# A three-block fp32 kernel: mixing in pieces, and the sparse attention's buffers, norm and last output moved to other steps

## The chip, the cores and the metric

The program runs on one core of one Trainium2 chip. Its time is the device time of one execution in microseconds (us). Before the change the median of three runs is 3529.36 us (3528.5 to 3529.94). The engines are TensorE (PE, with PEld for its weight loads), VectorE (DVE), ScalarE (ACT), GpSimd (POOL) and SyncE (SP, which issues the weight DMAs). Each runs its own instruction list in order, and they meet at semaphores.

## The reference, cut to what matters

```python
# first block, one layer: x is 512 x 1024
za, zb, zc, xbc, dt_raw, g_raw = split(rms_norm(h) @ w_in)
u, v  = split(gelu(za)); v = layer_norm(v)
ya    = u * (einsum('gts,bcsgd->bctgd', tril(w_s), v) + b_s)      # "mixing", 8 groups
yb    = gelu(gate) * scan(a, inp)   # a = exp(-8 * r * softplus(-lambda)), the "rate"
merged = gates[0] * (ya @ w_a) + gates[1] * (yb @ w_b) + gates[2] * (yc @ w_c)
# second block, two layers
x = x + 0.5 * swiglu(rms_norm(x), ffn1)
a_val, a_gate, b_gate, c_gate, b_h, q, k, v, q_idx, k_idx, w_idx = split(rms_norm(x) @ w_in)
y_a = silu(layer_norm(conv31(a_val * sigmoid(a_gate))))
y_b = b_gate * conv3(c_gate * b_h)
y_c = sparse_attention(q, k, v, top 128 keys of the indexer)     # 8 heads, 4 blocks of 128 queries
x = x + concat(y_a, y_b, y_c) @ w_out
x = x + cross_attention(rms_norm(x), rms_norm(mem))              # 256 memory rows, wk and wv from mem
x = x + 0.5 * swiglu(rms_norm(x), ffn2)
```

## The kernel before, in words

**Weights and panels.** Activations lie in SBUF with features on the partitions and the 512 positions along the row. Every weight matrix is worked off in panels of 128 output features. A panel is 24 matmuls (8 tiles of the contraction, three products each: high part by high part, high by low, low by high, since each fp32 value is held as two fp32r values). Two panels are a pair; `PHASES` lists all pairs in order. For panel k of the next pair ACT copies `raw` to `w_hi` (`prep`, L1183) once PE is through with panel k of this pair, and DVE forms `w_lo` (`prep_lo`, L1895). Before a panel PE waits for `w_lo` (`s_wlo`) and for the bank (`s_free`). So DVE has one panel of time for `w_lo`, less what ACT takes, and all its other work stands in order around these two steps.

**Buffers.** `xn_hi/xn_lo` hold a normed input, `y_hi/y_lo` an inner activation (in the first block the roles are the other way round; `b_hi/b_lo` is `xn`). `small`, `stat`, `rstd` and `arena` hold the rest. PSUM has the banks `G[0..3]` for panels and `B[0..3]` for other products.

**The gating phase.** The phases `u` (4 pairs, the half u of `za`), `lru0`, `lru1`, `ga0`, ... follow each other. `gmlp_norm(at_)` puts the layer norm of v beside the panels of `u` on DVE (variances at panel 3, division at 5, the tiles at 5 and 6). After the pair `lru0` PE runs `mix()` (L787): eight groups of four products. DVE turns each into `ya` with `mixed()`: an add (L2215), a product with u (L2220), ACT's copy of the high part (L1422), and the low part (L1910). Then DVE works out the recurrence's rate in small operations (`lru_rate`). POOL issues the DMA of the weights `lru_w` (L2569) when the low part of group 7 is done, since `lru_w` takes the place of u in the arena. PE's `lru_gates(0)` (L798) follows the pair `lru1` and waits for that DMA.

**The sparse attention.** Both layers run `MIX`, 22 panels of `w_in`, and beside them the indexer, the selection of keys for the blocks 1 and 2 (MAX8 and MATCH_REPLACE8 on DVE) and the taps of the convolution (product on ACT L1045, add on POOL L2582). Then comes a loop of 32 steps (4 query blocks by 8 heads), in `dsa_pe`, `dsa_act` and `dsa_dve`. In step i PE does the scores of step i+3 (L541), half a panel of the memory's keys or values (`half_kv`, L826, 12 matmuls), the output of step i (L581) and the transposes of the probabilities of step i+1 (L673). DVE does the maximum (L1774), `w_lo` in even steps and, until step 13, the selection for block 3; ACT does the exponential (L1078), `w_hi` in even steps and copies (L1089). Around this stand:
- the normed memory (`mem_hi` L1052, `mem_lo` L1753; 8 tiles each), at the start of the loop;
- per query block `out_tok` (L1787, DVE), `turn_out` (PE's transposes of it, L673, at head 1 of the next block), `out_hi` (L1129, ACT) and `out_lo` (L1910, DVE);
- the layer norm of the convolution: sums over channels in PE at step 19 and 21 (L553), the mean on DVE at step 20 (L1759 to L1764), square root on ACT at 23, reciprocal on DVE at 24 (L1827), Silu and high part on ACT at 25 (L1111, L1115), low part at 26.

After the loop the pairs of `w_out` (`mwo`) run as plain panels on `y_hi/y_lo`.

## Time and profile before

| | |
|---|---|
| median of 3 runs | 3529.36 us |
| profiled execution | 3529.81 us, span 3527.7 us |
| TensorE busy in the span | 3422.6 us (97%) |
| VectorE, ScalarE, GpSimd busy | 1958.6, 1360.1, 203.7 us |
| DMA | 310.29 MB, mean 88 GB/s |
| granted TensorE clock, mean | 0.989 of full speed |

The profile is one execution. Busy times are of instructions that compute. "L684" is line 684 of the kernel. A row of an instruction names what it writes, then what it reads, and behind its count the idle time before it and what ended that idle time. "PEclk" is the share of full speed that the clock of TensorE had in a stretch: 1.00 is 2.4 GHz, 0.50 is 1.2 GHz.

### The profile page before, as it was taken

The page shows a single profiled execution, that of the slowest core. Times are in us where ns is not written, and L with a number is a line of the kernel's source. Part 1 is how long each engine was busy: PE and PEld are TensorE (multiplying, and loading weights), DVE is VectorE, ACT ScalarE, POOL GpSimd, SP SyncE. Part 2 cuts the span into 40 slices and gives each one's busy share as a digit, 9 for nine tenths or more (in the row PEclk, how much of TensorE's full clock was granted, in tenths as well). Part 3 has the DMA queues.
Part 4 walks back from the last instruction along what each step waited for, and adds up shares of the span by engine and source line. Part 5 has one row for each costly group of instructions (what it writes and reads, how often), then busy time and mean ns, then how long its engine had stood idle before and what let it go on. Part 6 is the DMA issues. An engine that isn't in the chain of part 4 may idle for free.

```text
span 3527.7 us, 42389 instructions
## 1 busy us (share of the span) xinstructions
PE 3422.6 (97%) x15684; PEld 2783.7 (79%) x15684; DVE 1958.6 (56%) x2679; ACT 1360.1 (39%) x1915; POOL 203.7 (6%) x158
## 2 busy tenths in 40 slices
PE   7999999999999999999899999999999989999999
PEld 5778777888888888877678888888887777778887
DVE  4677765564446545588544544454446884454444
ACT  4455444432224342346534322342223564342223
POOL 1000000000000000045100000000000640000000
PEclk9999999999999999999999999999999999999999
DMA  4332312232223333322221333333333221223332
GB/s 129 94 84 84 96 48 72 96 111 96 95 96 96 96 95 96 90 84 72 72 72 60 96 95 96 90 101 96 98 94 89 84 72 60 72 72 95 96 96 83
DMA packets 425595, 310.29 MB, mean 88 GB/s; under 512 B 17256, under 2 KB 423200, under 8 KB 425440
## 3 DMA queue, kind: packets, MB, share of 16 engines
q1 hardware_dynamic: 422880, 302.13, 28.6%
q0 software_dynamic: 1664, 4.52, 0.4%
q8 instruction: 101, 1.65, 0.2%
q10 hardware_dynamic: 896, 1.54, 0.1%
q14 instruction: 54, 0.44, 0.0%
HBM read 306.06 MB, written 2.10 MB: 87 GB/s over the span
## 4 chain that ended last, share of the span: by engine, by line
PE 88%; DVE 8%; ACT 2%; issue 2%; DMA 0%; ACTq 0%; POOL 0%; DVEq 0%
PE G L684 75%; PE G L844 2%; PE G L826 2%; DVE arena L1744 1%; DVE w_lo L1895 1%; DVE small L1743 1%; PE B L673 1%; PE G L623 1%; PE B L604 1%; PE B L541 1%; PE B L581 1%; ACT w_hi L1183 1%; PE G L858 1%; PE G L673 0%; PE G L525 0%
## 5 line engine op out<-in xcount | busy, mean ns | idle before, releaser
L1183 ACT ACTIVATE w_hi<-raw 128x1024 fp32r<-128x1024 f32 x579 | 613.6, 1060 | 1523.3 <-PE G L684 1449.5
L1895 DVE TENSOR_TENSOR w_lo<-raw,w_hi 128x1024 fp32r<-128x1024 f32 x580 | 718.5, 1239 | 712.5 <-ACT w_hi L1183 710.0
L684 PE MATMUL G<-xn_hi,w_hi 128*128 128x512 f32 x2272 | 895.7, 394 | 12.1 <-DVE w_lo L1895 12.1
L684 PE MATMUL G<-xn_hi,w_lo 128*128 128x512 f32 x2272 | 885.8, 390 | 0.0
L684 PE MATMUL G<-xn_lo,w_hi 128*128 128x512 f32 x2272 | 885.4, 390 | 0.0
L684 PE MATMUL G<-y_hi,w_hi 128*128 128x512 f32 x1888 | 745.0, 395 | 3.4 <-DVE w_lo L1895 2.4
L684 PE MATMUL G<-y_hi,w_lo 128*128 128x512 f32 x1888 | 736.2, 390 | 0.0
L684 PE MATMUL G<-y_lo,w_hi 128*128 128x512 f32 x1888 | 735.7, 390 | 0.0
L684 PEld LDWEIGHTS G<-xn_hi,w_hi 128*128 128x128 f32 x2272 | 427.2, 188 | 118.2 <-issue 23.6
L684 PEld LDWEIGHTS G<-xn_lo,w_hi 128*128 128x128 f32 x2272 | 427.2, 188 | 91.3 <-issue 4.1
L684 PEld LDWEIGHTS G<-xn_hi,w_lo 128*128 128x128 f32 x2272 | 427.1, 188 | 89.7
L684 PEld LDWEIGHTS G<-y_hi,w_hi 128*128 128x128 f32 x1888 | 355.2, 188 | 85.9 <-issue 7.9
L684 PEld LDWEIGHTS G<-y_lo,w_hi 128*128 128x128 f32 x1888 | 355.2, 188 | 75.1 <-issue 2.9
L684 PEld LDWEIGHTS G<-y_hi,w_lo 128*128 128x128 f32 x1888 | 354.8, 188 | 74.6
L2582 POOL TENSOR_TENSOR arena<-arena,temps 128x512 f32<-128x512 f32 x90 | 132.3, 1483 | 1901.3 <-ACT temps L1045 1901.3
L1919 DVE SCALAR_TENSOR_TENSOR h<-G,h 128x512 f32 (+1 forms) x88 | 60.8, 691 | 254.8 <-PE G L684 254.8
L2025 DVE TENSOR_TENSOR temps<-G,rstd 128x512 f32<-128x512 f32 x88 | 60.8, 691 | 192.3 <-PE G L684 192.3
L1232 ACT ACTIVATE temps<-temps 128x512 f32<-128x512 f32 x88 | 55.6, 632 | 185.4 <-DVE temps L2021 185.4
L1936 DVE SCALAR_TENSOR_TENSOR h<-G,h 128x512 f32<-128x512 f32 x80 | 55.3, 691 | 120.6 <-PE G L684 112.5
L826 PE MATMUL G<-xn_hi,w_hi 128*128 128x256 f32 x256 | 84.9, 332 | 4.1 <-DVE xn_lo L1753 4.1
L1910 DVE TENSOR_TENSOR y_lo<-temps,y_hi 128x512 f32 (+1 forms) x124 | 83.5, 685 | 3.5 <-ACT y_hi L1235 3.1
L1235 ACT ACTIVATE y_hi<-temps 128x512 f32 (+1 forms) x88 | 55.7, 633 | 58.3 <-DVE temps L2028 58.3
(368 smaller groups left out, 3123.4 us busy)
## 6 DMA issues: line engine op xcount, KB each, us to landing
raw<-in_w_in SPq DMA_DIRECT2D x128, 512.0 KB, 4.3
raw<-in_ffn_w_gate SPq DMA_DIRECT2D x88, 512.0 KB, 4.0
raw<-in_ffn_w_up SPq DMA_DIRECT2D x88, 512.0 KB, 5.2
raw<-in_ffn_w_down SPq DMA_DIRECT2D x64, 512.0 KB, 4.2
raw<-in_w_mlp_up SPq DMA_DIRECT2D x32, 512.0 KB, 4.6
raw<-in_w_mlp_down SPq DMA_DIRECT2D x32, 512.0 KB, 4.1
raw<-in_xa_wkv SPq DMA_DIRECT2D x32, 512.0 KB, 4.1
raw<-in_w_out SPq DMA_DIRECT2D x24, 512.0 KB, 4.0
```

Of the source, the lines that this page charges most:

```text
L684: m = pe.matmul(bank[:, 0:n], a[:, k, kt, :], b[:, kt * S:kt * S + n], start=(kt == 0 and t == 0), stop=(kt == nk - 1 and t == 2))
L826: m = pe.matmul(G[k][:, 0:MEM], a[:, k, kt, :], b[:, kt * S:kt * S + MEM], start=(kt == 0 and t == 0), stop=(kt == KT - 1 and t == 2))
L844: m = pe.matmul(query_bank(l, k)[:, :], a[:, k, kt, :], b[:, kt * S:(kt + 1) * S], start=(kt == 0 and t == 0), stop=(kt == KT - 1 and t == 2))
L1183: act.activation(w_hi[:, k], raw[:, 1 - q, :, k * P:(k + 1) * P], ACT.Copy).then_inc(s_whi, 1)
L1232: act.activation(tmp(q), tmp(q), ACT.Silu).then_inc(s_yh, 1)
L1235: act.activation(cut(y_hi, i), tmp(2 + q), ACT.Copy).then_inc(s_yh, 1)
L1895: dve.tensor_tensor(w_lo[:, k], raw[:, 1 - q, :, k * P:(k + 1) * P], w_hi[:, k].bitcast(F32), ALU.subtract)\
L1910: return dve.tensor_tensor(dst, value, hi.bitcast(F32), ALU.subtract)
L1919: ins = dve.scalar_tensor_tensor(cut(h, 2 * i + k), G[2 * q + k][:, :], scale, cut(h, 2 * i + k), ALU.mult, ALU.add)
L1936: ins = dve.scalar_tensor_tensor(cut(h, j), G[2 * q + k][:, :], scale, cut(h, j), ALU.mult, ALU.add)
L2025: dve.tensor_tensor(tmp(4 + q), G[2 * q + 1][:, :], rstd[:, :], ALU.mult).then_inc(s_free, 1)
L2582: pool.tensor_tensor(acc, acc, tap_buffers[a % 4], ALU.add).then_inc(conv_p.sem, conv_p.mark("add", l, a))
```

## The change

**Gating phase.** `mix` takes a range of groups: 0 to 3 run after the last panel of `u`, 4 and 5 after the first panel of `lru0`, 6 and 7 after the second. DVE's `mixed` and ACT's `mixed_hi` take groups 0 to 2 at the end of `u`, 3 and 4 and then 5 and 6 beside `lru0`, and 7 beside `lru1`. The layer norm of v moves one panel earlier. The rate is worked out beside panel 1 of `u` and its exponential in phase `v`. POOL's DMA of `lru_w` waits for `y` of group 3 and not for the low part of group 7. `lru_gates(0)` moves from behind `lru1` to the middle of the pair `ga0`.

**Sparse attention.** The buffer of a normed input and that of an inner activation change roles at certain phases (`side_of`), so that the normed memory no longer lies where the input of `MIX` is; its 8 tiles are written beside the first four panels of `MIX`, two each. `turn_out` moves from head 1 to head 2, `out_hi` and `out_lo` from step 10 to 11 (18 to 19, 26 to 27); `out_tok` comes right behind the maximum in its step. The sums of the layer norm move from steps 19 and 21 to 20 and 23, the root from 23 to 25, Silu from 25 to 30; the high and low parts of `y_a` come behind the loop. The first pair of `mwo` is cut up by tiles: tiles 2 and 3 of panel 0, then the last `turn_out`, tiles 2 and 3 of panel 1, tiles 4 to 7 of both, tiles 0 and 1 of both.

```diff
+        def side_of(name):
+            if name[0] == "f":
+                l = int(name[3])
+                return l if name[1] == "1" else 1 - l
+            if name[:-1] in MIX:
+                return int(name[-1])
+            return 1 - int(name[-1]) if name[:-1] in ("xk", "xv", "mwo", "xq", "xo") else 0
+        def normed_for(name):
+            return (y_hi, y_lo) if side_of(name) else (xn_hi, xn_lo)
+        def inner_of(name):
+            return (xn_hi, xn_lo) if side_of(name) else (y_hi, y_lo)
...
-        mean_step, square_step, root_step, conv_y_step = 19, 21, 23, 25
+        mean_step, square_step, root_step = 20, 23, 25
...
-                    if hh == 1 and b:
+                    if hh == 2 and b:
                         turn_out(b - 1)
...
+            part_of_mixed(l, 0, (2, 3))
             turn_out(NB - 1)
+            part_of_mixed(l, 1, (2, 3))
+            for k in range(2):
+                part_of_mixed(l, k, (4, 5, 6, 7))
+            for k in range(2):
+                part_of_mixed(l, k, (0, 1))
+                values(0, k)
...
+                if (i, k) == (3, 1):
+                    mix(range(0, 4))
...
-                if (name, i) == ("lru", 0):
-                    mix()
-                if (name, i) == ("lru", 1):
-                    lru_gates(0)
+                     {("lru", 0): lambda i, k: mix(range(4 + 2 * k, 6 + 2 * k)),
+                      ("ga", 0): lambda i, k: None if k else lru_gates(0)}.get((name, i)))
...
+            def part_of_mixed(l, k, tiles):
+                n = P0[f"mwo{l}"]
+                if tiles[0] == 2:
+                    pe.wait_ge(s_free, n)
+                    pe.wait_ge(s_wlo, 2 * n + k + 1)
+                    pe.wait_ge(conv_v.sem, conv_v.at("short_lo", l, 1))
+                if tiles[0] == 4:
+                    pe.wait_ge(split_v.sem, split_v.at("dsa", l, NB - 1))
+                hi, lo = inner_of(f"mwo{l}")
+                for kt in tiles:
+                    if kt < 2:
+                        pe.wait_ge(conv_v.sem, conv_v.at("lo", l, kt))
+                    for t, (a, b) in enumerate(((w_hi, hi), (w_hi, lo), (w_lo, hi))):
+                        m = pe.matmul(G[2 * (n % 2) + k][:, :], a[:, k, kt, :], b[:, kt * S:(kt + 1) * S],
+                                      start=(kt == 2 and t == 0), stop=(kt == 1 and t == 2))
...
-            act.wait_ge(s_mm, 2 * P0[f"xk{l}"])
-            for j in range(KT):
-                mem_hi(j)
...
+                    if p < 4:
+                        for j in (2 * p, 2 * p + 1):
+                            mem_hi(act, l, j)
...
             for i in range(-3, len(steps)):
+                if i == square_step + 1:
+                    dve.wait_ge(full.sem, full.at("cln", l, 1))
...
-                if i == -2:
-                    for j in range(KT):
-                        mem_lo(j)
+                if i >= 8 and i % 8 == 0:
+                    out_tok(i // 8 - 1)
...
-                if i >= 10 and (i - 10) % 8 == 0:
-                    out_lo((i - 10) // 8)
+                if i >= 11 and (i - 11) % 8 == 0:
+                    out_lo((i - 11) // 8)
...
+                if at_ == 7:
+                    mixed((0, 1, 2))
...
+                if name == "lru" and i < 2:
+                    mixed(((3, 4), (7,))[i])
+                if (name, i) == ("lru", 1):
+                    lru_conv(0)
                 prep_lo(n, q, 1)
...
-            pool.wait_ge(gmlp_v.sem, gmlp_v.at("lo", 7))
+            pool.wait_ge(gmlp_v.sem, gmlp_v.at("y", 3))
```

On VectorE, in the gating phase, the rows before run from `w_lo` of `lru0` to the first groups of the mixing (L2215 and L2220 are a group's add and product, L1910 its low part):

```order
L1895 TENSOR_TENSOR w_lo<-raw,w_hi 128x1024 x3
L2215 TENSOR_TENSOR temps<-B,arena 128x512
L2220 TENSOR_TENSOR temps<-temps,arena 128x512
L2215 TENSOR_TENSOR temps<-B,arena 128x512
L2220 TENSOR_TENSOR temps<-temps,arena 128x512
L1910 TENSOR_TENSOR xn_lo<-temps,xn_hi 128x512
L2215 TENSOR_TENSOR temps<-B,arena 128x512
L2220 TENSOR_TENSOR temps<-temps,arena 128x512
L1910 TENSOR_TENSOR xn_lo<-temps,xn_hi 128x512
```

After the change the same place reads as follows (L1953 is `w_lo`, L2243 and L2248 are add and product, L1968 the low part):

```order
L1953 TENSOR_TENSOR w_lo<-raw,w_hi 128x1024 x2
L2243 TENSOR_TENSOR temps<-B,arena 128x512
L2248 TENSOR_TENSOR temps<-temps,arena 128x512
L2243 TENSOR_TENSOR temps<-B,arena 128x512
L2248 TENSOR_TENSOR temps<-temps,arena 128x512
L1968 TENSOR_TENSOR xn_lo<-temps,xn_hi 128x512
L2243 TENSOR_TENSOR temps<-B,arena 128x512
L2248 TENSOR_TENSOR temps<-temps,arena 128x512
L1968 TENSOR_TENSOR xn_lo<-temps,xn_hi 128x512 x2
L1953 TENSOR_TENSOR w_lo<-raw,w_hi 128x1024
L2243 TENSOR_TENSOR temps<-B,arena 128x512
L2248 TENSOR_TENSOR temps<-temps,arena 128x512
```

Groups 0 to 2 now stand one `w_lo` earlier, and a `w_lo` stands behind them where all eight groups followed each other.

On ScalarE, in the sparse attention, the rows before around Silu at step 25 are these (L1111 Silu, L1115 its high part, L1078 the exponential, L1183 `w_hi`, L1089 a copy of transposed probabilities):

```order
L1078 ACTIVATE arena,small<-arena,small 128x512
L1089 ACTIVATE arena<-G 128x512
L1111 ACT_TABLE_LOAD
L1111 ACTIVATE arena<-arena,par 128x512 x2
L1115 ACTIVATE y_hi<-arena 128x512 x2
L1078 ACT_TABLE_LOAD
L1078 ACTIVATE arena,small<-arena,small 128x512
L1183 ACTIVATE w_hi<-raw 128x1024
L1089 ACTIVATE arena<-G 128x512
```

After the change Silu (L1158) stands behind the last exponential, at the end of the loop (L1230 `w_hi`, L1136 the copy, L1113 the copy of a key panel, L1176 `out_hi`, L1163 the high part of `y_a`):

```order
L1230 ACTIVATE w_hi<-raw 128x1024
L1136 ACTIVATE arena<-G 128x512
L1113 ACTIVATE arena<-G 128x256
L1158 ACT_TABLE_LOAD
L1158 ACTIVATE arena<-arena,par 128x512 x2
L1176 ACTIVATE xn_hi<-B 128x4x128
L1163 ACTIVATE xn_hi<-arena 128x512 x2
```

No exponential follows it there, and one table load is gone; `out_hi` of the last block now stands behind it.

## Rows read from the trace of the kernel before

**Rows 1.** The page: span and busy times.

```profile
span 3527.7 us, 42389 instructions
PE 3422.6 (97%) x15684; PEld 2783.7 (79%) x15684; DVE 1958.6 (56%) x2679; ACT 1360.1 (39%) x1915; POOL 203.7 (6%) x158
```

**Rows 2.** Busy time by stretch: length, then each engine's, granted clock, DMA.

```profile
180.00:1540.00 1360.00, 1353.18 (x6009) 1096.92 (x6008) 800.34 (x990) 515.35 (x624) 6.70 (x6) 1.00 0.30 90
135.00:172.00 37.00, 31.35 (x152) 25.38 (x150) 28.08 (x51) 16.07 (x22) 2.34 (x3) 0.91 0.32 86
1640.00:1790.00 150.00, 132.51 (x780) 103.85 (x779) 89.83 (x178) 82.41 (x176) 24.49 (x18) 0.92 0.20 64
2840.00:2990.00 150.00, 132.01 (x782) 104.18 (x781) 91.10 (x179) 82.35 (x177) 24.15 (x17) 0.92 0.20 64
```

**Rows 3.** Timeline of PE in the gating phase: start, length, instruction, idle before.

```profile
142.65 5.72 PE L787 MATMUL B<-arena 128*128 128x128 f32 x48
149.26 1.16 PE L787 MATMUL B<-arena 128*128 128x128 f32 x8 [0.89 <-DVE temps L2215]
...
168.82 3.39 PE L798 MATMUL B<-arena 128*128 128x512 f32 x4 [3.86 <-DMA arena<-in_lru_w_i]
```

**Rows 4.** Timeline of DVE in the gating phase: `w_lo` and an add.

```profile
128.62 1.22 DVE L1895 TENSOR_TENSOR w_lo<-raw,w_hi 128x1024 fp32r<-128x1024 f32 x1
...
148.52 0.69 DVE L2215 TENSOR_TENSOR temps<-B,arena 128x512 f32<-128x512 f32 x1
```

**Rows 5.** Waits of PE between 140 and 215 us: total, times, longest.

```profile
PE B L787 <- DVE temps L2215: 1.8, 2, 0.9
PE B L798 <- DVE arena L2245: 1.1, 1, 1.1
```

**Rows 6.** Timeline of PE in the sparse attention of layer 0: its waits.

```profile
1649.13 0.55 PE L826 MATMUL G<-xn_hi,w_hi 128*128 128x256 f32 x1 [1.90 <-DVE xn_lo L1753]
...
1671.58 0.70 PE L541 MATMUL B<-arena 64*128 64x256 f32 x2 [1.28 <-DVE small L1774]
...
1681.89 0.63 PE L673 MATMUL B<-consts,rstd 128*128 128x128 f32 x4 [2.10 <-DVE rstd L1787]
...
1715.02 1.98 PE L553 MATMUL B<-arena,consts 128*128 128x512 f32 x4 [1.28 <-DVE y_lo L1910]
...
1726.45 2.84 PE L553 MATMUL B<-temps,consts 128*128 128x512 f32 x4 [2.61 <-DVE temps L1764]
...
1758.19 1.34 PE L581 MATMUL B<-arena 128*128 128x64 f32 x8 [2.35 <-ACT arena L1089]
...
1775.16 0.63 PE L673 MATMUL B<-consts,rstd 128*128 128x128 f32 x4 [1.11 <-DVE rstd L1787]
```

**Rows 7.** Timeline of DVE and ACT there: memory tiles, `w_lo` beside POOL, table load.

```profile
1648.49 3.26 DVE L1753 SCALAR_TENSOR_TENSOR xn_lo<-arena,par,xn_hi 128x256 fp32r<-128x256 f32 x8
...
1667.56 2.10 DVE L1895 TENSOR_TENSOR w_lo<-raw,w_hi 128x1024 fp32r<-128x1024 f32 x1
1669.58 0.68 DVE L1743 MAX8 small<-arena 128x8 f32<-128x512 f32 x1
...
1747.78 3.34 DVE L1827 RECIPROCAL stat<-stat 128x512 f32<-128x512 f32 x1
```

**Rows 8.** Timeline of ACT around the root and Silu.

```profile
1742.70 1.28 ACT L1078 ACT_TABLE_LOAD   x1
1744.00 0.72 ACT L1078 ACTIVATE arena<-arena,small 128x512 f32<-128x512 f32 x1
```

**Rows 9.** Busy time in stretches at the half clock, as rows 2.

```profile
1683.83:1687.24 3.41, 3.41 (x17) 3.08 (x16) 0.38 (x3) 1.72 (x4) 1.28 (x1) 0.50 0.00 0
1728.20:1731.61 3.41, 3.41 (x14) 2.85 (x13) 0.05 (x2) 0.00 (x0) 0.00 (x0) 0.50 0.02 5
1758.92:1765.75 6.83, 6.83 (x26) 5.00 (x26) 3.20 (x7) 2.50 (x6) 0.00 (x0) 0.50 0.46 154
...
1775.99:1779.40 3.41, 3.41 (x10) 2.62 (x9) 0.69 (x1) 0.43 (x1) 0.00 (x0) 0.50 0.60 209
```

More of the change, by code:

```diff
@@ L675, in turn, with panel @@
                 m.then_inc(full.sem, full.mark(*key))
-            def panel(k, bank, hi, lo, nk, n, ready=None):
+            def panel(k, bank, hi, lo, tiles, n, ready=None):
                 m = None
-                for kt in range(nk):
+                for kt in tiles:
                     if ready:
@@ L776, in gmlp_turns, with mix @@
                         turn(("v", j), [vt[:, j * S + t * P:j * S + (t + 1) * P] for t in range(NB)], (gmlp_a, ("v", j)))
-            gemm("u", normed, unroll=True, after=gmlp_turns)
-            def mix():
+                if (i, k) == (3, 1):
+                    mix(range(0, 4))
+            def mix(groups):
                 pe.wait_ge(gmlp_v.sem, gmlp_v.at("normed", NB - 1))
-                for g in range(8):
+                for g in groups:
                     bank = take(("mix", g), (gmlp_v, ("mixed", g)))
@@ L789, in mix @@
                     m.then_inc(full.sem, full.mark("mix", g))
+            gemm("u", normed, unroll=True, after=gmlp_turns)
             def lru_gates(jj):
@@ L873, in panel_of_gb @@
                 pe.wait_ge(s_wlo, 2 * n + k + 1)
-                panel(k, G[k], *(branch if k else normed), KTS["gb"], S).then_inc(s_mm, 1)
+                panel(k, G[k], *(branch if k else normed), tile_order("gb", i), S).then_inc(s_mm, 1)
             pe.wait_ge(s_free, P0["gb"] - 1)
@@ L980, in values @@
                                             for d in range(2) for t in range(2)], (xa_v, ("xv", l, j)))
-                gemm(f"mwo{l}", y, unroll=True, ready=mixed_ready, after=values)
+                dsa_pe(pe, l, take, turn, half_kv, rotate, part_of_mixed, values)
+                wide(False)
+                for i in range(1, 4):
+                    n = P0[f"mwo{l}"] + i
+                    pair(f"mwo{l}", i, n, n % 2, inner_of(f"mwo{l}"), inner_of(f"mwo{l}"), S, after=values)
                 for x in range(4):
@@ L1128, in out_hi @@
             act.wait_ge(full.sem, full.at("ot", l, b))
-            act.activation(block_of(y_hi, b), out_bank(l, b), ACT.Copy).then_inc(split_a.sem, split_a.mark("dsa", l, b))
+            act.activation(block_of(inner_of(f"mwo{l}")[0], b), out_bank(l, b), ACT.Copy).then_inc(split_a.sem, split_a.mark("dsa", l, b))
         def cross_act(act, l, prep):
@@ L1253, in norm_tile @@
                 if gain:
-                    act.activation(cut(xn_hi, j), cut(h, j), ACT.Copy, scale=col(gain, g0 + j))\
+                    act.activation(cut(norm_buffers(r)[0], j), cut(h, j), ACT.Copy, scale=col(gain, g0 + j))\
                        .then_inc(norm_a.sem, norm_a.mark("hi", r, j))
@@ L1366, in _, with mixed_hi @@
                         act.activation(small[:, 0:4], small[:, 0:4], ACT.Sqrt).then_inc(gmlp_a.sem, gmlp_a.mark("std"))
+            def mixed_hi(groups):
+                for g in groups:
+                    act.wait_ge(gmlp_v.sem, gmlp_v.at("y", g))
+                    act.activation(cut(b_hi, g), tmp(4 + g % 2), ACT.Copy).then_inc(gmlp_a.sem, gmlp_a.mark("hi", g))
+            mixed_hi((0, 1, 2))
             def lru_inputs(j):
```

194 lines of the change are left out of this document (101 added, 93 removed).

## The prediction

> **What bounds the kernel now.** The page comes first: PE is busy for 97% of the span, 3422.6 of 3527.7 us, and DVE for 56% [rows 1]. So PE is the limit, and only two things can give time back: gaps in PE, and stretches in which PE works at its lower clock. The windows tell where these are. From 180 to 1540 us PE is busy for 1353.2 of 1360 us at the full clock, though that holds all of the first block behind the gates [rows 2]; nothing can be won there. In the gating phase, 135 to 172 us, PE is idle for 5.65 of 37 us and the mean clock is 0.91, which is 37 x 0.09 = 3.3 us lost. In the sparse attention of layer 0, 1640 to 1790 us, PE is idle for 17.5 of 150 us with 0.92, which is 12 us lost, and in that of layer 1 for 18.0 us with 0.92 as well [rows 2].
>
> Third, the timelines of PE, with the idle time and its releaser behind each row. In the gating phase PE waits for DVE's add of the mixing (twice 0.9 us) and then 3.86 us for the weights of the gates [rows 3, 5]. In a layer of the sparse attention the waits of the change's steps are 1.90 (DVE's low parts of the memory), 1.28 (the maximum, late because of them), 2.10 (`turn_out`, for `out_tok`), 1.28 (`out_lo`), 2.61 (the mean of the layer norm), 2.35 (the copy of probabilities, behind Silu) and 1.11 (`turn_out` again) [rows 6]. Fourth, short windows at the half clock: 3.41, 3.41, 6.83 and 3.41 us long, at 1683.83, 1728.20, 1758.92 and 1775.99 [rows 9]. Each begins within 2 us of the end of one of those waits, and PE is full in them.
>
> **The change, part by part: the gating phase.** The mixing's 48 matmuls take 5.72 us, so a group of 8 takes 0.95 [rows 3]. DVE needs per group an add of 0.69 [rows 4], and a product and a low part of the same shape, 2.1 us in all. Before, PE issued eight groups in a row, 7.6 us, against 17 us of DVE's work, ran out of banks and waited twice. Now four groups stand behind `u` and the others two at a time behind a panel of `lru0`. Three of a panel's 24 matmuls are a tile; the panels between the pieces give DVE some 5.4 us each for two groups (4.2) and a `w_lo` (1.22 [rows 4]). That just fits, since DVE may trail by the four banks. The two waits, 1.8 us, go.
>
> The DMA of `lru_w` waited for the low part of group 7 and now waits for the product of group 3; it is issued about 20 us earlier, and the gates come a panel later. The wait of 3.86 us goes. Both half-clock stretches of that phase (3.3 us together) follow these waits, and go with them. The rate's small operations move to panel 1 of `u`, where DVE has nothing else but a `w_lo`: nothing. The layer norm of v moves a panel up, which squeezes the `w_lo` of the last panels of `u`: I charge 0.25 us. `lru_gates(2)` waits 1.1 us for the convolution L2245 [rows 5]; with its surroundings shifted I add 0.9. Sum: 1.8 + 3.86 + 3.3 - 0.25 - 0.9 = **7.8 us**. Bounds: 3.86 + 1.8 - 1.15 = 4.5 without the clock, and 9.0 with no new wait.
>
> **The start of the sparse attention.** The normed memory no longer lies where the input of `MIX` lies, so its 8 tiles go beside `MIX`'s first four panels, where a panel of PE lasts 5.4 us and DVE has little beside a `w_lo` of 1.22; two tiles take 0.8. PE waited 1.90 for these low parts. DVE spent 3.26 us on them [rows 7] and is then continuously busy with the selection until step 10, so it is 3.26 us earlier all the way, and the wait 1.28 for the maximum goes too. Of 3.2 I take 3.0. A half-clock stretch at the very start stays, since the waits for the first scores ahead of it stay.
>
> **Output of a block.** `turn_out` at head 2, behind an `out_tok` that stands first in its step: the wait 2.10 goes. Moving `out_hi`/`out_lo` along leaves the distance to their readers, so of the sums' 1.28 only 0.3 goes. Later blocks give 0.4. In all 2.8.
>
> **The convolution's norm.** The square sums move from two to three steps behind the first: the wait of 2.61 goes. Silu with its two table loads held ACT between two exponentials: the wait of 2.35 goes. The load is 1.28 us and the next activation begins 1.30 us after the load's start [rows 8], so the load has no tail. The end of the loop now holds the reciprocal (3.34 us [rows 7]) two steps later, nearer the last exponentials, and `out_lo` of block 3 behind Silu. The cover is the first pair of `mwo`: tiles 2 and 3 of a panel are 6 matmuls, 1.36 us, and there are two such parts before `y_c` of block 3 is read. Of the 1.8 us waits at the tail (one is the 1.11) I let 1.25 come back: 0.55 gained. In all 2.61 + 2.35 + 0.55 = 5.5.
>
> (The Trainium skill, "ScalarE: Activation LUTs", section "What ACT_TABLE_LOAD costs", gives a switch of table set a load of about 1283 ns and a pipeline drain of about 1380 ns. The trace agrees on the load and shows no drain: 1742.70 + 1.28 = 1743.98, and the activation starts at 1744.00 [rows 8]. By the page the load ahead of Silu would hold the last `out_hi`, which is now behind it, 1.4 us longer in each layer, and the time would be 2.8 us later, 3488.3. By the row it is 3485.5, and the row decides.)
>
> **Clock.** Waits gone: 3.0 + 2.8 + 5.5 = 11.3 us per layer. Four half-clock stretches go with them: 3.41 + 3.41 + 6.83 + 3.41 = 17.06 us [rows 9], in which PE did 8.5 us of full-clock work. Layer 1 has the same mean clock [rows 2]. The smaller waits that stay or arise may bring one stretch of 3.41 back, 1.7 us. So a layer gives 11.3 + 8.5 - 1.7 = **18.1 us**. Bounds: below, 11.3 with no clock at all; above, 11.3 + 8.5 + 1.9 (half of the start's waits) = 21.7.
>
> The cutting of the first `mwo` pair adds no matmul. Its tiles 0 and 1 stand last because `y_a` comes behind the loop: high and low parts of two tiles, four operations of about 0.7 us on ACT and DVE, against twelve matmuls times two, 5.4 us, of cover. Nothing.
>
> **Sum.** 7.8 + 2 x 18.1 = 44.0. The profiled execution took 3529.81 us, 2.1 beside its span, and the median is 0.45 lower. 3529.81 - 44.0 - 0.45 = 3485.4; I say **3485.5**. Own range: 3529.4 - 9.0 - 43.4 = 3477 to 3529.4 - 6 - 2 x 15.5 = 3492.
>
> **Rivals.**
>
> *The waits go, the clock stays.* If the half-clock stretches have another cause than the waits, or the many waits under 1 us that stay call them up, the gain is 7.8 - 3.3 + 2 x 11.3 = 27: 3502. For it: in [rows 9] PE is full in the stretches. Against it: each begins right behind a wait of at least 1.1 us, and 1360 us without waits have clock 1.00 [rows 2].
>
> *DVE keeps its debt.* DVE is busy for 89.8 of 150 us there [rows 2], most of it up to step 13, where the selection ends. If the 3.26 us freed are eaten by waiting for `w_hi` and for scores, and `out_tok` ahead of the other work in its step makes a `w_lo` late, the 3.0 turns to 1.5 and half of 2.8 goes, with one stretch more staying: 1.5 + 1.4 + 1.7 = 4.6 less, so 13.5 per layer. Time 3529.4 - 7.8 - 27 = 3494.6.
>
> *The mixing gives nothing.* If DVE, with `w_lo` between the groups, trails by more than four banks, PE waits at the pieces or at `w_lo` what it waited before: 3485.5 + 7.8 = 3493.3.
>
> *Slower: buffers that hold DVE.* One `w_lo` beside POOL's add (both read two operands from SBUF) took 2.10 us against 1.22 alone [rows 4, 7]. Moving the DVE's work by some us changes which of it meets POOL's 17 or so adds. If it were to meet the selection, 16 steps of MAX8 and MATCH_REPLACE8 with 0.7 each would double: 16 x 1.4 = 22 us, all on the path while DVE is the limit, and seven `w_lo` 0.9 each, 6.3. Then a layer loses 28 and gains 18: 3529.4 - 7.8 + 2 x 10 = 3542. It decides once the selection's operations pass some 1.2 us: then a layer loses 16 us and more, about what the rest gains. Against it: MAX8 reads one operand and is 0.68 at 1669.58, right behind the stretched `w_lo` [rows 7]. (The Trainium skill, "SBUF — State Buffer", section "Who interferes with whom", says that a DVE instruction with two SBUF inputs and a GpSimd one that reads SBUF shut each other out for a whole instruction, and that one with at most one SBUF input doesn't contend. The stretched `w_lo` agrees with the first half. By it the new memory tiles, two inputs each, could each be held by an add when they meet one beside `MIX`; by the row that is at most 0.9 us of DVE's idle time there. It also leaves MAX8, with its one operand, out of this rival's doubling, as the row does, and that is why the chance is small.)
>
> **Chances.** Forecast 0.57; clock stays 0.12; DVE keeps its debt 0.17; mixing gives nothing 0.10; slower 0.04. The range takes in the bounds of the first, and the means of the second to fourth: 3477 to 3503. Under 0.2% is 7 us, about what a measurement tells from no change; no case ends there, and I leave it 0.02. Faster 0.94, slower 0.04.
>
> **What would show it.** Right: no PE wait over 0.5 us at the mixing (L787's successor), none on a DMA before the gates, which start in the pair `ga0`; windows of 150 us in both layers with PE idle 6 to 7 us and clock at 0.97 or more; no DVE instruction of the memory behind `MIX`; no wait of PE over 1.2 us between the first scores and the first panels of `mwo`. Wrong: clock still 0.92 with PE idle 6 us (clock stays); PE waits on the maximum or `out_tok` above 1.5 us (DVE's debt); a wait on `mixed`'s add or `w_lo` in `lru0` over 1 us each (mixing); MAX8 over 1.2 us (slower). The forecast fails as a whole if a wait of over 2 us appears at the end of the loop, where reciprocal, root and Silu now stand close together.

## The result and the profile after

The changed kernel takes 3484.09 us (median of 4 runs, 3482.78 to 3484.82); the kernel before took 3529.65 us beside it (3528.5 to 3531.03). The ratio is 0.987, 95% interval [0.9853, 0.9887]: 45.6 us less, where 44 were forecast. Run once more in the last comparison it gave 3484.19 us (3483.32 to 3484.68).

The page after, span and busy times:

```profile
span 3483.0 us, 42388 instructions
PE 3403.2 (98%) x15684; PEld 2769.2 (80%) x15684; DVE 1958.7 (56%) x2679; ACT 1354.9 (39%) x1911; POOL 205.8 (6%) x158
```

Against [rows 1], PE's idle time fell from 3527.7 - 3422.6 = 105.1 to 79.8 us, 25.3 less, and its busy time by 19.4 us with the same 15684 matmuls. So a little less than half of the gain is matmuls at a higher clock, as forecast (27.1 us of waits, 16.9 of clock). But 2.5 of the 19.4 us stand at the end of the program, which the change doesn't touch. Behind the last panel the same 24 matmuls stand in both kernels. In the kernel before most of them fell into a half-clock stretch, in the changed one none did (before, then after, up to the end of the span; the 25th is the end of the panel's last):

```profile
3514.75:3527.74 12.99, 5.35 (x25) 4.98 (x24) 4.90 (x10) 4.11 (x6) 0.00 (x0) 0.58 0.41 161
```

```profile
3471.22:3483.02 11.80, 2.83 (x24) 2.62 (x24) 4.72 (x10) 4.12 (x6) 0.00 (x0) 0.87 0.45 178
```

Windows of the changed kernel, the same stretch of the gating phase and 150 us of each sparse attention (length, then busy time of PE, PEld, DVE, ACT, POOL, granted clock, DMA share, GB/s), answering to [rows 2]:

```profile
135.00:172.00 37.00, 37.00 (x182) 30.70 (x181) 27.12 (x38) 16.22 (x23) 2.34 (x3) 1.00 0.43 114
...
1625.00:1775.00 150.00, 142.61 (x860) 112.21 (x859) 98.63 (x183) 85.30 (x177) 29.59 (x21) 0.98 0.22 72
...
2810.00:2960.00 150.00, 143.01 (x864) 112.97 (x863) 100.06 (x186) 84.02 (x176) 28.99 (x20) 0.98 0.22 71
```

In the gating phase PE has no gap left, and the clock is full. In the two layers it is idle for 7.4 and 7.0 us where it was for 17.5 and 18.0, at 0.98 for 0.92.

Timeline of PE after in layer 0, the rows with a wait, answering to [rows 6] (start, length, instruction, idle time before it and its releaser):

```profile
1634.47 0.46 PE L562 MATMUL B<-arena 64*128 64x128 f32 x2 [2.37 <-DVE arena L1774]
...
1637.55 0.76 PE L562 MATMUL B<-arena 64*128 64x128 f32 x2 [1.16 <-DVE small L1835]
...
1661.22 0.70 PE L562 MATMUL B<-arena 64*128 64x256 f32 x2 [1.18 <-DVE small L1835]
...
1703.94 1.98 PE L574 MATMUL B<-arena,consts 128*128 128x512 f32 x4 [0.95 <-DVE xn_lo L1968]
...
1743.35 1.10 PE L602 MATMUL B<-arena 128*128 128x64 f32 x8 [0.71 <-ACT arena L1136]
...
1748.31 1.10 PE L602 MATMUL B<-arena 128*128 128x64 f32 x8 [0.69 <-ACT arena L1136]
...
1762.39 0.47 PE L712 MATMUL G<-xn_hi,w_hi 128*128 128x512 f32 x1 [0.30 <-DVE w_lo L1953]
```

The waits for the low parts of the memory (1.90), for `out_tok` (2.10 and 1.11) and for the mean (2.61) are gone. Two have hardly moved: the maximum (1.28, now 1.18) and `out_lo` (1.28, now 0.95). Of the half-clock stretches [rows 9] none of the four is left, and none of layer 1's between its loop's start and 2995 us. Three stay, in part in one layer only: one in `MIX`, one behind `mwo`, and the one at the loop's start. That last one, in each kernel:

```profile
1646.28:1653.11 6.83, 4.74 (x17) 3.77 (x17) 6.72 (x18) 2.97 (x8) 0.83 (x1) 0.50 0.13 45
```

```profile
1636.74:1643.56 6.82, 6.01 (x19) 4.27 (x19) 5.84 (x16) 1.54 (x7) 1.46 (x1) 0.50 0.23 80
```

The first row is before, the second after. PE now works through 6.01 us of it where it worked for 4.74 and waited for the rest: a wait removed inside such a stretch is worth half here, since the 1.27 us of matmuls that fill it run at the half clock and would take 0.64 at the full one.

Landmarks split the 44.7 us of span by stage. The first scores of layer 0 come at 1634.47, and the second pair of `mwo` starts at 1762.39. The same two rows of the kernel before:

```profile
1643.38 0.46 PE L541 MATMUL B<-arena 64*128 64x128 f32 x2 [2.37 <-DVE arena L1716]
...
1788.97 0.47 PE L684 MATMUL G<-y_hi,w_hi 128*128 128x512 f32 x1
```

So 8.9 us come from the gating phase and 26.6 in all by the second place, of which layer 0 gave 17.7. The second pair of `mwo` of layer 1 starts at 2944.32, before at 2987.77: layer 1 gave 16.9. The last 1.2 us are those of the end. Layer 1 gave less than layer 0 although more waiting went there, since a half-clock stretch in its `MIX`, behind a wait of 4.34 us for `w_lo` that both kernels have, is twice as long after as before (before, then after):

```profile
2772.70:2776.10 3.40, 2.87 (x7) 2.32 (x8) 3.26 (x9) 0.00 (x0) 3.40 (x3) 0.50 0.01 2
```

```profile
2746.10:2752.90 6.80, 6.19 (x15) 4.87 (x16) 6.52 (x15) 0.00 (x0) 5.32 (x4) 0.50 0.00 1
```

One number ahead of the prediction was wrong: `MIX` has 26 panels, not 22. Nothing was worked out from it.

### The profile page after: what moved, and what is told of

Its sections match the earlier page's. It is cut to its first block, busy times and chain, and to the rows that moved or that the text cites. A ratio compares the mean times of both kernels' runs of the same rounds, so it can differ in the third digit from the quotient of the medians.

```text
span 3483.0 us, 42388 instructions
## 1 busy us (share of the span) xinstructions
PE 3403.2 (98%) x15684; PEld 2769.2 (80%) x15684; DVE 1958.7 (56%) x2679; ACT 1354.9 (39%) x1911; POOL 205.8 (6%) x158
## 4 chain that ended last, share of the span: by engine, by line
PE 89%; DVE 7%; ACT 1%; issue 1%; DMA 0%; ACTq 0%; DVEq 0%
PE G L712 75%; PE G L878 2%; PE G L859 2%; DVE w_lo L1953 1%; DVE arena L1802 1%; PE B L701 1%; DVE small L1801 1%; PE B L562 1%; PE B L602 1%; PE G L651 1%; PE B L632 1%; PE G L912 1%; ACT w_hi L1230 1%; PE G L897 1%; PE B L979 0%
## 5 line engine op out<-in xcount | busy, mean ns | idle before, releaser
L1230 ACT ACTIVATE w_hi<-raw 128x1024 fp32r<-128x1024 f32 x579 | 613.6, 1060 | 1506.3 <-PE G L712 1419.4
L1953 DVE TENSOR_TENSOR w_lo<-raw,w_hi 128x1024 fp32r<-128x1024 f32 x580 | 718.8, 1240 | 675.6 <-ACT w_hi L1230 673.1
L712 PE MATMUL G<-y_hi,w_hi 128*128 128x512 f32 x2320 | 916.8, 395 | 9.2 <-DVE w_lo L1953 8.2
L712 PE MATMUL G<-y_hi,w_lo 128*128 128x512 f32 x2320 | 904.6, 390 | 0.0
L712 PE MATMUL G<-y_lo,w_hi 128*128 128x512 f32 x2320 | 904.2, 390 | 0.0
L712 PE MATMUL G<-xn_hi,w_hi 128*128 128x512 f32 x1808 | 711.0, 393 | 6.8 <-DVE w_lo L1953 6.8
L712 PE MATMUL G<-xn_hi,w_lo 128*128 128x512 f32 x1808 | 704.3, 390 | 0.0
L712 PE MATMUL G<-xn_lo,w_hi 128*128 128x512 f32 x1808 | 704.1, 389 | 0.0
L712 PEld LDWEIGHTS G<-y_hi,w_hi 128*128 128x128 f32 x2320 | 436.3, 188 | 113.5 <-issue 17.5
L712 PEld LDWEIGHTS G<-y_hi,w_lo 128*128 128x128 f32 x2320 | 436.2, 188 | 91.5
L712 PEld LDWEIGHTS G<-xn_hi,w_hi 128*128 128x128 f32 x1808 | 339.8, 188 | 90.0 <-issue 14.6
L712 PEld LDWEIGHTS G<-xn_lo,w_hi 128*128 128x128 f32 x1808 | 339.9, 188 | 72.1 <-issue 2.4
L712 PEld LDWEIGHTS G<-xn_hi,w_lo 128*128 128x128 f32 x1808 | 339.7, 188 | 70.8
```

The costliest lines, as they stand in the source:

```text
L712: m = pe.matmul(bank[:, 0:n], a[:, k, kt, :], b[:, kt * S:kt * S + n], start=(kt == tiles[0] and t == 0), stop=(kt == tiles[-1] and t == 2))
L1230: act.activation(w_hi[:, k], raw[:, 1 - q, :, k * P:(k + 1) * P], ACT.Copy).then_inc(s_whi, 1)
L1953: dve.tensor_tensor(w_lo[:, k], raw[:, 1 - q, :, k * P:(k + 1) * P], w_hi[:, k].bitcast(F32), ALU.subtract)\
```

## The experiments

Each kernel ran on the same chip beside the kernel before, in 4 timed runs (`before_early_dma` in 10). The measured number is the median. "Changed kernel" is 3484.1 us. The kernel before took 3530.1, 3528.2 and 3529.6 us beside the three sets of experiments, so a difference against a kernel of another set is good to some 2 us.

**The gating phase put back (`gating_back`).** All hunks of `mix`, `mixed`, the rate, `lru_gates` and the DMA as before:

```diff
-                if (i, k) == (3, 1):
-                    mix(range(0, 4))
...
+                if (name, i) == ("lru", 0):
+                    mix()
+                if (name, i) == ("lru", 1):
+                    lru_gates(0)
...
-            pool.wait_ge(gmlp_v.sem, gmlp_v.at("y", 3))
+            pool.wait_ge(gmlp_v.sem, gmlp_v.at("lo", 7))
```

> The changed kernel with the gating phase as before; the sparse attention as changed. If a lost wait gives back its own time and the half-clock stretch behind it: 3484.1 + 8.9 = 3493 us (8.9 us is how much earlier PE reaches the first scores of layer 0 after the change, 1634.47 against 1643.38), with waits of 0.9, 0.9 and 3.9 us and two half-clock stretches back. If the waits alone counted: 3484.1 + 5.2 = 3489.3. If the gating phase's gain is given away later: 3484 to 3486.

Measured: 3493.6 us (3491.7 to 3498.0), 9.5 more. PE's waits are back as they were, and the two stretches at the half clock behind the second and the third of them:

```profile
148.65 1.16 PE L819 MATMUL B<-arena 128*128 128x128 f32 x8 [0.90 <-DVE temps L2266]
...
150.70 1.79 PE L819 MATMUL B<-arena 128*128 128x128 f32 x8 [0.90 <-DVE temps L2266]
...
168.20 3.61 PE L830 MATMUL B<-arena 128*128 128x512 f32 x4 [3.80 <-DMA arena<-in_lru_w_i]
```

The phase's gain is real, carries through the 3300 us behind it, and needs the clock to be explained: the waits alone would have given 3489.3, and the lowest of the four runs is 3491.7. That lowest one is the profiled execution, 6.9 us longer than the changed kernel's: 5.2 of waits, and half of 3.4 us, since two half-clock stretches came back and one in layer 1's `MIX` was shorter by 3.4.

**The DMA of `lru_w` alone (`before_early_dma`).** The kernel before with one edit:

```diff
-            pool.wait_ge(gmlp_v.sem, gmlp_v.at("lo", 7))
+            pool.wait_ge(gmlp_v.sem, gmlp_v.at("y", 3))
```

> The kernel before, where POOL's DMA of lru_w waits for y of group 3 and not for the low part of group 7, nothing else. The DMA starts about 8 us earlier (four groups of 2.1 us). If it alone ends the wait of 3.86 us: 3529.5 - 3.9 - 1.7 (the stretch behind it) = 3524; waits alone 3525.6. The two waits of 0.9 us in the mixing stay. If the DMA is the kind that is slowed by the weights' traffic and the wait only moves: 3527 to 3530.

Measured: 3529.2 us (3525.0 to 3530.9, 10 runs), ratio 1.0005 [0.9995, 1.0014]: nothing. POOL issues the DMA at 151.92 instead of 161.89, and it takes 5.6 us to land, so the weights are there before 159. The gates start at 168.31 all the same. PE and DVE in that kernel:

```profile
168.31 2.04 PE L798 MATMUL B<-arena 128*128 128x512 f32 x2 [5.30 <-issue]
```

```profile
162.15 0.17 DVE L2075 TENSOR_SCALAR small<-small 128x8 f32<-128x8 f32 x1 [0.92 <-ACT small L1426]
...
165.30 0.54 DVE L2242 TENSOR_SCALAR arena<-arena,par 128x512 f32<-128x512 f32 x1
165.88 2.33 DVE L2245 SCALAR_TENSOR_TENSOR arena<-arena,par 128x512 f32<-128x512 f32 x3
```

The releaser has become "issue", which names nobody. The row that ends where the gates begin (165.88 + 2.33 = 168.21) is the convolution of group 0, which stood in DVE's order behind all of the mixing and the rate's small operations. In the kernel before the same row stands at 166.39 and ends at 168.72, a tenth of a us before the gates start [rows 3]; the DMA issued at 162.79 lands 5.7 us later, at 168.5. So two things were late together, and the profile named one of them. The change moves both: `mixed` in pieces, the rate to panel 1 of `u`, and the gates a panel later. How much each of these three does wasn't run.

**The normed memory at the start of the loop again (`mem_late`)** (in its new buffers):

```diff
-                    if p < 4:
-                        for j in (2 * p, 2 * p + 1):
-                            mem_lo(dve, l, j)
...
+                if i == -2:
+                    for j in range(KT):
+                        mem_lo(dve, l, j)
```

(and `mem_hi` on ACT likewise)

> The changed kernel, but the normed memory's 8 tiles are written at the start of the loop as before (in the new buffers). By the prediction's step (1.90 and nearly all of 1.28 us go): two layers of 3.0 us, 3490.1. By the two traces (1.90 and 0.10 us of waits gone, 0.95 us lost again since PE now works through the half-clock stretch in which it waited before): two layers of 1.05, 3486.2, with the wait for the low parts near 1.9 us and the one for the maximum near 1.3.

Measured: 3489.9 us (3488.0 to 3491.5), 5.8 more. The waits in layer 0 are 1.89 for the low parts, 1.28 and 0.22 for the maximum, as the traces said. The median is that of the first expectation. The profiled run, the fastest of the four, has a span of 3486.2 us, 3.2 more than the changed kernel's, and in these two executions the half-clock stretches ahead of the program's end add up to the same 27.3 us. So with an equal clock the memory's move is worth 1.6 us a layer; how much of the rest up to 2.9 is its own and how much is scatter (3.5 us between the four runs) stays open.

Why the wait for the maximum hardly fell is in DVE's rows of the changed kernel, at the start of the loop:

```profile
1642.11 0.68 DVE L1802 MATCH_REPLACE8 arena<-small,arena 128x512 f32<-128x512 f32 x1
1643.89 0.29 DVE L1835 CUSTOM_DVE_ANT_0 arena<-B,consts 128x128 f32<-128x128 f32 x1 [1.10 <-issue]
...
1646.64 1.23 DVE L1953 TENSOR_TENSOR w_lo<-raw,w_hi 128x1024 fp32r<-128x1024 f32 x1 [0.53 <-ACT w_hi L1230]
```

DVE got 3.26 us, then waited 1.10 us and 0.53 for `w_hi`: half of what it was given. In the kernel before it has no such wait between 1650 and 1672 us. The 1.10 are put down to "issue"; PE's scores at 1643.02 take 0.73 us and so end at 1643.75, 0.14 ahead of the maximum, and PE has worked at its half clock up to 1643.56. So it is most likely PE's slow start that limits DVE's lead; no run without that stretch shows it.

**`turn_out` at head 1 again (`turn_head1`):**

```diff
-                    if hh == 2 and b:
+                    if hh == 1 and b:
...
-                if i >= 11 and (i - 11) % 8 == 0:
+                if i >= 10 and (i - 10) % 8 == 0:
```

(the last two lines in ACT and in DVE)

> The changed kernel, but turn_out at head 1 and out_hi and out_lo a step earlier, as before; out_tok still stands right behind the maximum. If the move of turn_out is what counts: wait 2.1 us at the first turn_out, 0.4 at the third, and a half-clock stretch (1.7 us) back in each layer, 4.2 x 2: 3492.5 (waits without the clock: 3489.1). If the place of out_tok on DVE is what counts (it comes a w_lo and a selection round earlier, 1.2 + 1.4 us): no wait over 0.3 us, and 3484 to 3485.

Measured: 3490.2 us (3486.9 to 3492.9), 6.1 more, but by neither way. No wait for `out_tok` is there, and none for `out_lo` at the sums. So the place of `out_tok` on DVE, ahead of `w_lo` and a selection round, is enough to take the 2.10 us away; whether the move of `turn_out` alone would do it too wasn't run. What is new is at the reciprocal (PE, DVE and ACT of this kernel):

```profile
1743.87 1.10 PE L602 MATMUL B<-arena 128*128 128x64 f32 x8 [1.85 <-ACT arena L1136]
```

```profile
1735.65 0.69 DVE L1968 TENSOR_TENSOR xn_lo<-B,xn_hi 128x512 fp32r<-128x512 f32 x1
1736.26 3.34 DVE L1885 RECIPROCAL stat<-stat 128x512 f32<-128x512 f32 x1
```

```profile
1741.57 0.72 ACT L1125 ACTIVATE arena<-arena,small 128x512 f32<-128x512 f32 x1 [4.30 <-DVE small L1835]
```

`out_lo` of block 2 stands in the step of the reciprocal, the next maximum comes 0.6 us later, and the exponential behind it waits 4.30 us. In the changed kernel it comes a step later, and PE waits 0.71. A half-clock stretch follows the 1.85, none the 0.71. Head 2 is right, but because of what it does at step 26. (In the profiled execution the waits that differ come to little: 1.14 more here and 0.95 less at the sums in each layer. Most of its 7.2 us over the changed kernel's is clock: its half-clock stretches ahead of the program's end add up to 44.4 us, for 27.3. Two of 3.41 are those behind the 1.85; the others stand or are longer behind waits that both kernels have.)

**The square sums a step earlier (`square_22`):**

```diff
-        mean_step, square_step, root_step = 20, 23, 25
+        mean_step, square_step, root_step = 20, 22, 25
```

> The changed kernel, but the square sums two steps behind the first sums (20 and 22, before 19 and 21; now 20 and 23). If waits take a half-clock stretch with them: a wait of 2.6 us and 1.7 us of clock per layer, 3484.1 + 8.6 = 3492.7. Waits alone: 3489.3. If the step after 20 is free enough by itself: below 3486.

Measured: 3483.9 us (3483.7 to 3485.0): no change. The distance between the two sums, to which the prediction gave the 2.61 us, is worth nothing.

**The norm's steps one later in the kernel before (`before_mean20`):**

```diff
-        mean_step, square_step, root_step, conv_y_step = 19, 21, 23, 25
+        mean_step, square_step, root_step, conv_y_step = 20, 22, 24, 26
```

> The kernel before, with the four steps of the convolution's norm one later (20, 22, 24, 26 for 19, 21, 23, 25), nothing else. The run with the square sums at 22 left the time unchanged, so the third step between the sums is not what took the wait away. Theory: the mean stood in an even step of DVE, behind w_lo, which waits for w_hi (2.2 us idle at 1723.03); in an odd step it starts right behind the maximum. Then the wait of 2.61 us goes here too, with its half-clock stretch: 3529.5 - 2 x 4.3 = 3521, and the first sums no longer wait 1.28 us for out_lo: up to 2 x 1.3 more. Rival (the distance counts, or the freed time is lost at Silu in the next even step): 3527 to 3530.

Measured: 3508.4 us (3507.4 to 3509.6), ratio 0.995 [0.9934, 0.9967]: 19.7 us less than the kernel before beside it (3528.2), over two fifths of the whole change by four numbers, and twice what was expected. DVE before, around the mean, and in the run with the square sums at 22:

```profile
1723.03 1.22 DVE L1895 TENSOR_TENSOR w_lo<-raw,w_hi 128x1024 fp32r<-128x1024 f32 x1 [2.20 <-ACT w_hi L1183]
1724.17 0.68 DVE L1759 TENSOR_SCALAR stat<-B 128x512 f32<-128x512 f32 x1
```

```profile
1710.66 0.68 DVE L1835 CUSTOM_DVE_ANT_0 arena<-B,arena 128x512 f32<-128x512 f32 x1
...
1711.27 0.69 DVE L1820 TENSOR_SCALAR stat<-B 128x512 f32<-128x512 f32 x1
```

In an even step the mean stands behind `w_lo`, which waits 2.20 us for `w_hi`; in an odd step it follows the maximum at once. The steps' parity was the cause of the 2.61. Three waits of a layer go with it (1.28 for `out_lo`, 2.61, 0.42), and the one beside Silu falls from 2.35 to 1.46:

```profile
1756.18 1.10 PE L581 MATMUL B<-arena 128*128 128x64 f32 x8 [1.46 <-ACT arena L1089]
```

The expectation had missed the last two. (All four steps moved together here, the reciprocal's too, so how much of these two is the mean's isn't separated.) PE's idle time fell by 9.7 us and its busy time by 12.4 (page of that kernel: span 3505.6, PE 3410.2).

**Silu at step 27 (`silu_27`):**

```diff
-                if i == len(steps) - 2:
+                if i == 27:
```

> The changed kernel, but Silu of the convolution runs in ScalarE's step 27, two steps behind the root, as before, and not in step 30; high and low parts stay behind the loop. If Silu with its two table loads (1.28 each, Silu 1.52: 4.1 us between two exponentials) is what made PE wait 2.35 us before: that wait less the 0.7 that is there now, and 3.4 us of clock, come back in each layer: 3484.1 + 2 x 5.0 = 3494. Waits alone: 3487.4. If the reciprocal on DVE (3.34 us) was the cause and Silu only stood in its shadow: 3484 to 3486.

Measured: 3496.1 us (3488.8 to 3496.5), 12 more; the profiled run is the fastest, and the other three lie within 0.8 us. Its mean granted clock was 0.995, that of the other three 0.992 and 0.993, and 0.0025 of 3490 us is 8.7. So by this estimate their 7 to 8 us more are clock, lost in places that no profile shows. The profiled run alone is 4.0 us above the changed kernel's. PE waits 2.33 us where it waited 0.71:

```profile
1744.79 1.11 PE L602 MATMUL B<-arena 128*128 128x64 f32 x8 [2.33 <-ACT arena L1136]
```

```profile
1738.22 1.28 ACT L1158 ACT_TABLE_LOAD   x1
1739.67 1.52 ACT L1158 ACTIVATE arena<-arena,par 128x512 f32<-128x512 f32 x2 [0.17 <-DVE arena L1887]
1741.21 1.28 ACT L1125 ACT_TABLE_LOAD   x1
1742.50 0.72 ACT L1125 ACTIVATE arena<-arena,small 128x512 f32<-128x512 f32 x1
```

The exponential comes at 1742.50 for 1741.05 in the changed kernel. So Silu between two exponentials costs 1.5 us here (PE waits 1.6 more); the other 0.7 are there without it, behind the reciprocal. As the rows behind [rows 8] did, these show the load alone: 1741.21 + 1.28 = 1742.49, and the exponential starts at 1742.50. (The Trainium skill's drain of about 1380 ns, "ScalarE: Activation LUTs", "What ACT_TABLE_LOAD costs", does not appear in either place.)

**The first pair of `mwo` uncut (`uncut`):**

```diff
-            part_of_mixed(l, 0, (2, 3))
             turn_out(NB - 1)
-            part_of_mixed(l, 1, (2, 3))
-            for k in range(2):
-                part_of_mixed(l, k, (4, 5, 6, 7))
             for k in range(2):
+                part_of_mixed(l, k, (2, 3))
+                part_of_mixed(l, k, (4, 5, 6, 7))
                 part_of_mixed(l, k, (0, 1))
```

> The changed kernel, but the first pair of mwo is not cut between its panels: the last turn_out first, then panel 0 whole, then panel 1. From the trace: PE would reach the last turn_out at 1749.4 and the tokens' output is ready at 1750.3, then 0.3 us for out_lo: 1.2 us per layer, 3486.5; with a half-clock stretch behind it 3489.9. If the cut is worth nothing: 3484 to 3485.

Measured: 3488.4 us (3488.0 to 3492.7), 4.3 more. The wait for the last `out_tok` is back with the very length that it had before, in both layers:

```profile
1751.30 0.63 PE L699 MATMUL B<-consts,rstd 128*128 128x128 f32 x4 [1.11 <-DVE rstd L1846]
```

Six matmuls, 1.36 us, ahead of `turn_out` cover it. The 0.30 for `w_lo` behind it doesn't arise in this kernel, so the cut is worth 0.8 us of waiting a layer. No half-clock stretch stands behind the 1.11 here, in either layer, though 0.69 stands ahead of it as in the kernel before. In the profiled execution one stretch of 3.41 us more than the changed kernel's stands elsewhere, 1.7 us. 1.6 and 1.7 make up 3.3 of the 3.5 by which that execution is longer.

**Two edits for a faster kernel, and both with a third.** In the changed kernel PE's longest wait in a layer is 4.34 us for a `w_lo` in `MIX`, behind four rounds of the selection on DVE. Then come 3.14 at the first panels that read the normed stream behind `mwo` (L878, for DVE's L2599), which no run here shortens, and 2.37 at the first scores. `select_spread`:

```diff
+        for p in range(13, 17):
+            del selections[p]
+        selections |= {14 + j: (2, range(3 * j, min(16, 3 * j + 3))) for j in range(6)}
```

> The changed kernel, with the 16 selection rounds of query block 2 spread over panels 14 to 19 of MIX, three each, for four each on panels 13 to 16. DVE's four rounds of 1.25 us at panel 13 stand ahead of the w_lo for which PE waits 4.34 us in each layer (two smaller waits of 0.4 and 0.3 follow). All of it gone: 2 x (4.34 + 0.67) and two half-clock stretches of 1.7 us or more: 3484 - 10 - 3.4 = 3470.6. Waits alone 3474. If the debt arrives later, at the index heads of block 3 or the first scores: 3480 to 3484.

Measured: 3473.9 us (3473.2 to 3476.9), ratio to before 0.985 [0.9833, 0.9866]; no run of it comes within 6 us of one of the changed kernel beside it. The 4.34 us is gone in both layers, 0.16 is left there and 0.75 later (for 0.4 and 0.3), and the half-clock stretch behind it is gone:

```profile
span 3471.4 us, 42390 instructions
PE 3399.6 (98%) x15684; PEld 2764.9 (80%) x15684; DVE 1958.7 (56%) x2679; ACT 1354.2 (39%) x1911; POOL 208.9 (6%) x158
```

```profile
1561.34 0.47 PE L715 MATMUL G<-xn_hi,w_hi 128*128 128x512 f32 x1 [0.16 <-DVE w_lo L1956]
...
1594.12 0.50 PE L715 MATMUL G<-xn_hi,w_hi 128*128 128x512 f32 x1 [0.75 <-DVE w_lo L1956]
```

The expectation was 3470.6 with the clock and 3474 for the waits alone. It lands on the second, though both stretches went; 0.75 us of waiting came back. This is the fastest version here, and beats both kernels. The other edit, `rope_first`:

```diff
-                    prep_lo(n, q, k)
+                    if p < 25:
+                        prep_lo(n, q, k)
...
+                if i == -2:
+                    n = P0[f"k{l}"] + 1
+                    prep_lo(n, n % 2, 1)
```

> The changed kernel, with DVE's w_lo at the last panel of MIX moved behind the first two maxima and the late rotation. In the trace DVE waits 1.72 us for w_hi there, while the rotation that PE's first scores wait for (2.37 us) is queued behind it. PE's wait should fall to about 0.9, 1.5 us per layer: 3481. If the half-clock stretch at the loop's start goes with it, 3.4 us more per layer: 3474. If DVE's debt is only moved to the next maximum: 3484.

Measured: 3485.9 us (3485.3 to 3486.9), 1.7 slower than the changed kernel beside it. The wait fell to 0.94 as expected, and came back:

```profile
1633.82 0.46 PE L562 MATMUL B<-arena 64*128 64x128 f32 x2 [0.94 <-DVE arena L1774]
...
1642.74 0.76 PE L562 MATMUL B<-arena 64*128 64x128 f32 x2 [1.86 <-DVE small L1835]
...
1650.34 0.46 PE L562 MATMUL B<-arena 64*128 64x128 f32 x2 [1.42 <-DVE small L1835]
```

DVE is behind there, so a `w_lo` moved later delays the next maxima. This is the case in which the debt is only moved.

All three edits together, `all_three`:

> Both edits, and in the gating phase DVE's convolution of channel group 2 ahead of the scan of group 1, for which lru_gates(2) waits 1.45 us. Sum of the waits: 3 + 10 + 1.45 = 14.5: 3469.6, with the clock stretches behind them to 3460. If they overlap: the better of the two single runs, about 3471.

Measured: 3476.7 us (3475.9 to 3480.3), worse than `select_spread` alone. The third edit puts `lru_conv(2)` ahead of `lru_scan(1)`; the wait of 1.45 us becomes one of 0.94 for the `w_lo` behind it. `rope_first` costs more than it did alone (all three edits take 2.8 us more than `select_spread`, where it took 1.7 more than the changed kernel): PE waits 3.88 us for a maximum at 1645.07, for 1.42 there.

The changed kernel beside them, `after_again`:

> The changed kernel itself, run beside the next ones. 3482 to 3486, as in the first comparison; what it scatters is what the experiments are to be read against.

Measured: 3484.2 us, as above.

## Why the prediction was right, step by step

**The view.** That PE's gaps and its half-clock stretches are the only two places for a gain held: 25.3 and 19.4 us of the span (2.5 of the latter at the program's end, by luck). One reading for it was wrong: the prediction calls the 1360 us from 180 to 1540 "without waits". PE is idle there for 6.8 us, in single waits of up to 1.47 us (at 440.11), and the clock stayed full; so not every wait over 1.1 us takes the clock with it.

**Gating phase, 7.8 forecast, 8.9 seen** by the landmark, 9.5 by putting it back. The waits that went are 1.8 + 3.86; `lru_gates(2)` waits 1.45 for 1.11, not the 2.0 allowed, and a `w_lo` 0.17: 5.15. The two stretches are 3.4. The cause of the 3.86 was told in half. The prediction named the DMA, and the gates a panel later, but not the convolution; `before_early_dma` shows that the earlier DMA ends nothing alone, with the convolution just as late. It is issued at 145.53, 16.4 us earlier and not 20.

**Start of the sparse attention, 3.0 forecast.** By the waits 1.90 + 0.10 = 2.0 in layer 0, less half of the 1.27 us that now run in the slow stretch, so 1.4. This term of the sum was too large: it let all of DVE's 3.26 us reach the maximum. `mem_late` gives 1.6 a layer by its span, at an equal clock, and 2.9 by its median.

**Output of a block, 2.8 forecast, 2.85 in the waits** (2.10, 0.33 and 0.42). The size was right, the cause in part: `out_tok` ahead of `w_lo` is enough for it, and what head 2 was seen to do is to keep `out_lo` away from the reciprocal.

**The norm, Silu and the tail, 5.5 forecast, 5.06 in the waits.** 2.61 went; of 2.35 + 0.69 + 1.11 there remain 0.71 + 0.69 + 0.30. The step that fails is the reason for the 2.61: "the square sums move from two to three steps" was undone at no cost, and the parity of the mean's step is what counts. Silu's place was worth 1.6 us of waiting a layer (`silu_27`), not the whole 2.35: 0.7 us of it stay without Silu, behind the reciprocal. The cut of the first `mwo` pair, which the prediction used as cover for 1.25 us that would return, did its work: 0.81 us a layer were gained, for 0.55, and by `uncut` 1.11 less 0.30 hang on it.

**Clock, 8.5 less 1.7 forecast.** All four stretches of 17.06 us went (8.5), and no new one came in layer 0, so the 1.7 was not needed there; 0.6 was lost in the stretch at the start. Together 9.9 + 7.9 = 17.8 us in layer 0, where the landmarks say 17.7, against 18.1 forecast. Waits a little too large and clock a little too small cancelled. In layer 1 the 1.7 did come, in the longer stretch of `MIX`, and the layer gave 16.9. So 8.9 + 17.7 + 16.9 = 43.5 us of the span are the change's, and 1.2 the end's, which nobody forecast: that the sum is off by so little is in part luck. The own range takes 6 and 15.5 for its slow end, where the bounds worked out are 4.5 and 11.3; nothing is given for that, and the stated 3503 comes from the rivals.

**The rivals.** The waits go, the clock stays: excluded by 19.4 us of busy time, or 16.9 without the end. DVE keeps its debt: half true at the start, by 1.4 to 1.6 us of the 3.0 a layer. The mixing gives nothing: excluded by `gating_back`. Buffers that hold DVE: `w_lo` beside POOL's add took 2.23 us at 1657.07, for 2.10 before, and MAX8 stayed at 0.69; no selection was stretched (the longest of all 96 MAX8 took 0.70 us, of all MATCH_REPLACE8 0.68). (That agrees with the rule of the Trainium skill, "SBUF — State Buffer", "Who interferes with whom".)

What stays open: the size of the memory's term beyond 1.6 us a layer, since the scatter of `mem_late` (3.5 us) and of `turn_head1` (6 us) is larger than that of the changed kernel (2 us). Part of the scatter can be seen. The changed kernel was profiled twice, and the same wait of 3.14 us stands in both layers of both executions. In the first execution (`after`) a half-clock stretch follows it in layer 1 only, in the second (`after_again`) in layer 0 only. The 3.4 us behind it, layer 0 and then layer 1, first in `after`, then in `after_again`:

```profile
1812.30:1815.70 3.40, 3.40 (x15) 2.83 (x16) 0.53 (x1) 0.00 (x0) 0.00 (x0) 1.00 0.81 269
...
2995.30:2998.60 3.30, 3.30 (x10) 2.52 (x9) 0.00 (x0) 0.00 (x0) 0.00 (x0) 0.50 0.90 305
```

```profile
1813.00:1816.40 3.40, 3.40 (x10) 2.64 (x9) 0.00 (x0) 0.00 (x0) 0.00 (x0) 0.50 0.84 290
...
2995.30:2998.70 3.40, 3.40 (x15) 2.83 (x16) 0.51 (x1) 0.00 (x0) 0.00 (x0) 1.00 0.84 268
```

So the same wait costs 1.7 us more or not, and differences of 2 to 4 us between two profiled kernels can be of this kind. Why it is the one or the other isn't shown.

## What to carry to other kernels

A wait behind which the clock falls costs its own length and half of the slow stretch behind it; look for both, and price a wait inside a slow stretch at half. Whether the clock falls behind a given wait can differ from one execution to the next, so compare the sum of the half-clock stretches before a few us are put down to an edit. The releaser in a profile is the last of several: before an edit is credited with a wait, look on every engine for a row that ends at the same time, and change one of them alone. In a hand-written schedule the order of two operations within a step, and whether a step is one with the weights' work, can be worth more than a whole buffer: 20 us for four numbers in the kernel before, 10 us for spreading 16 rounds evenly, and 3 to 6 for the memory's new place.
